# Recurrence queries, two sparse-attention projections and eight gate tiles by seven products, their weight sums on GpSimd

## The reference, cut to what matters

```python
(sq, sk, sv, dq, dk, dv, iq, ik, iw, hq, hf, hi, hg,
 g_sb, g_dsa, g_hg) = jnp.split(h @ w_in_l, _split_points(), axis=-1)
y_sb = stick_breaking_attention(heads(sq, N_SB), heads(sk, N_SB), heads(sv, N_SB)) @ w_sb_l   # 6 heads of 64
y_dsa = dsa_attention(q, k, dv, q_i, k_i, iw) @ w_dsa_l        # 64 best keys of each query, by a score of 8 index heads
o = hgrn2(heads(hq, N_HG), heads(hf, N_HG), heads(hi, N_HG), lb)   # recurrence, 4 heads; q = silu(hq), f = lb + (1 - lb) sigmoid(hf)
y_hg = (rms_norm(o, onorm) * silu(hg)) @ w_hg_l
mixed = sigmoid(g_sb) * y_sb + sigmoid(g_dsa) * y_dsa + sigmoid(g_hg) * y_hg
return mixed @ w_out_l
```

## Time and profile before

| | us |
|---|---|
| median of 3 runs | 1598.62 (1598.06 to 1599.4) |
| the profiled execution | 1599.52 |
| its span, first to last instruction | 1597.7 |
| TensorE busy | 1465.1 (92%) |
| VectorE, ScalarE, GpSimd busy | 740.9, 314.8, 22.7 |
| mixer of layer 0, from the first "hf" product | 79.8 to about 249 |
| mixer of layer 1 | about 552 to 719 |
| mean granted TensorE clock | 0.957 |

### The profile page before, as it was taken

How to read it: one execution, slowest core, us unless ns; L and a number is a source line. 1 busy time by engine, 2 the same in 40 slices (tenths; PEclk the granted TensorE clock), 3 DMA queues, 4 the chain that set the end, 5 groups by cost and what they waited for, 6 DMA issues and landing times.

```text
span 1597.7 us, 19690 instructions
## 1 busy us (share of the span) xinstructions
PE 1465.1 (92%) x8156; PEld 1006.0 (63%) x8156; DVE 740.9 (46%) x1465; ACT 314.8 (20%) x655; POOL 22.7 (1%) x41
## 2 busy tenths in 40 slices
PE   8999999999999999999999999999999576576578
PEld 5587889999544788898999445755554133133132
DVE  3646576766666646567666656544331000001001
ACT  2234431122001125430222001334410000000000
POOL 0000000000000000000000002200000000000000
PEclk9999999999999999999999999999999788788789
DMA  9547224454443633334444446755799999999997
GB/s 321 187 159 237 95 101 153 161 182 179 158 167 110 218 130 135 106 106 158 158 161 181 186 158 196 232 185 184 288 381 425 427 427 425 428 427 426 427 419 313
DMA packets 114921, 380.17 MB, mean 238 GB/s; under 512 B 10836, under 2 KB 23252, under 8 KB 104144
## 3 DMA queue, kind: packets, MB, share of 16 engines
q1 hardware_dynamic: 111952, 369.53, 60.7%
q0 software_dynamic: 2880, 9.36, 1.9%
HBM read 377.25 MB, written 5.73 MB: 240 GB/s over the span
## 4 chain that ended last, share of the span: by engine, by line
PE 32%; DMA 17%; SPq 1%; DVE 0%; ACT 0%; issue 0%; DVEq 0%
DMA ring<-in_w 17%; PE bank L1495 6%; PE bank L1541 6%; PE bank L1151 4%; PE bank L1692 4%; PE bank L1261 2%; PE bank L1590 2%; PE bank L1718 1%; SPq L928 1%; PE bank L1751 1%; PE bank L1187 1%; PE bank L1213 1%; PE bank L1200 1%; PE bank L1714 1%; PE bank L1648 0%; PE bank L1681 0%
## 5 line engine op out<-in xcount | busy, mean ns | idle before, releaser
L1144 PE MATMUL bank<-hT,ring 128*128 128x256 f32 x832 | 185.4, 381 | 0.0
L1144 PEld LDWEIGHTS bank<-hT,ring 128*128 128x128 f32 x832 | 156.0, 190 | 21.9 <-issue 1.0
L1692 PE MATMUL bank<-ring,region 128*32 128x512 f32 x208 | 115.7, 720 | 50.2 <-DMA region<-in_w 50.2
L1692 PE MATMUL bank<-region 128*32 128x512 f32 x512 | 115.8, 720 | 42.9 <-DMA ring<-in_w 42.9
L1541 PE MATMUL bank<-region 128*128 128x512 f32 x320 | 140.6, 592 | 0.0
L1541 PEld LDWEIGHTS bank<-region 128*128 128x128 f32 x320 | 60.5, 190 | 74.6 <-issue 74.6
L1495 PE MATMUL bank<-region 128*128 128x128 f32 x768 | 100.5, 275 | 0.0
L1495 PEld LDWEIGHTS bank<-region 128*128 128x128 f32 x768 | 93.0, 192 | 0.0
L1692 PEld LDWEIGHTS bank<-region 128*32 128x32 f32 x512 | 28.8, 129 | 87.4 <-issue 87.4
L1692 PEld LDWEIGHTS bank<-ring,region 128*32 128x32 f32 x208 | 25.7, 129 | 85.0 <-issue 85.0
L1751 PE MATMUL bank<-region 128*32 128x512 f32 x192 | 61.9, 748 | 15.7 <-DMA hT<-in_w 13.9
(11 more groups left out here) (486 smaller groups left out, 2413.7 us busy)
## 6 DMA issues: line engine op xcount, KB each, us to landing
region<-in_w SPq DMA_DIRECT2D x43, 2048.0 KB, 38.6
ring<-in_w SPq DMA_DIRECT2D x30, 2048.0 KB, 37.5
ring<-in_w_in SPq DMA_DIRECT2D x26, 2048.0 KB, 8.4
ring<-in_w_up SPq DMA_DIRECT2D x16, 2048.0 KB, 8.3
ring<-in_w_down SPq DMA_DIRECT2D x32, 1024.0 KB, 6.4
own_slot<-in_w SPq DMA_DIRECT2D x7, 2048.0 KB, 43.5
ring<-in_w_out SPq DMA_DIRECT2D x6, 2048.0 KB, 7.8
region<-in_w SPq DMA_DIRECT2D x22, 512.0 KB, 9.0
```

What stands on the lines that cost most here:

```text
L1144: t = mm(b[:, 0:T], w[:, k, :], act[:, k, :], start=(k == 0), stop=(k == KD - 1))
L1692: t = mm(b[32 * e:32 * e + 32, :], xg[:, k, 32 * e:32 * e + 32], four[e][c][:, 512 * (k % 2):512 * (k % 2) + 512], start=(k == 0), stop=(k ...
```

## The change

`hq` (two groups), `sk` and `sq` together (three groups, with `sk` as one half of the columns and `sq` as the other) and the gates 2 and 3 (four groups) are made by seven products. That leaves eight plain gate tiles a layer. `em` is one product of such an early group, `ec` ScalarE's copy of m1 and VectorE's four sums, `ef` what is then made of the corners. All early groups share one tile of corners in the own slot. The weight sums of all 13 groups (the late gates too) are made by GpSimd, in order, in two sets of tiles by turns, a set when the group two before is done. In the levels, 0, 2, 4 and 6 now hold a group each and level 1 one plain tile; 3 and 5 hold none. `ge` makes the tokens' sums for the gates 2 and 3 behind `ln`. `attT` is cleared behind the second `tk` and no longer in `hp`. GpSimd's sums of the first five groups stand ahead of its t5 and bias transfers, the others behind.

```diff
-LATE_GATES = 8
+PLAIN_GATES, LATE_GATES = 8, 8
+GROUPS = (("hq", 0), ("hq", 1), ("skq", 0), ("skq", 1), ("skq", 2),
+          (2, 0), (2, 1), (3, 0), (3, 1), (4, 0), (4, 1), (5, 0), (5, 1))
+EARLY, IN_HEADS = 9, 5
+POOL_SUM = {"m5": 1, "m6": 3, "m7": 3, "m3": 4}
...
+    def em(n):
+        return [("em", n, m) for m in GATE_ORDER] + [("ec", n), ("ef", n)]
...
-    s += gm("hf", 1, *GATE_ORDER) + [("gc", "hf", 1), ("gf", "hf", 1), ("hq", 0)]
-    s += [("rt", c) for c in range(9)] + [("hj",)] + [("hq", m) for m in range(1, 4)]
+    s += gm("hf", 1, *GATE_ORDER) + [("gc", "hf", 1), ("gf", "hf", 1)]
+    s += [("rt", c) for c in range(9)] + [("hj",)] + em(0) + em(1)
     s.append(("hp",))
     half = N_IDX // 2
-    s += [("ix", 0, j) for j in range(half)] + [("sk", 0)] + [("ix", 0, j) for j in range(half, N_IDX)] + [("tk", 0)]
-    s += [("sk", m) for m in (1, 2)] + [("sq", m) for m in range(3)] + [("t5",)]
+    s += [("ix", 0, j) for j in range(half)] + em(2) + [("ix", 0, j) for j in range(half, N_IDX)] + [("tk", 0)]
+    s += em(3) + em(4) + [("t5",)]
     s += [("ix", 1, j) for j in range(N_IDX)] + [("tk", 1)]
-    s += [("z", c) for c in range(3)] + g(2) + [("ln",)] + g(2)
+    s += [("z", c) for c in range(3)] + g(2) + [("ln",), ("ge",)] + g(2)
...
-        s += g(2 if j < 2 else 1)
-
-    s += [("gt",), ("gw", 4), ("ho",)]
+        s += em(5 + j // 2) if j % 2 == 0 else g() if j == 1 else []
+
+    s += [("gt",), ("ho",)]
...
+            def weight_sums(l, n):
+
+                G = nc.gpsimd
+                for c in {"hq": ("hq",), "skq": ("sk", "sq")}.get(GROUPS[n][0], (("g", GROUPS[n][0]),)):
+                    pool.wait_ge(*arrive[chunk_at[(l, c)]])
+                if n == 0:
+                    pool.wait_ge(*bk.full((l, "rsb")))
+                elif n == 1 and l == 0:
+                    pool.wait_ge(kv_stored, 16)
+                elif n >= 2:
+                    pool.wait_ge(*group_done(l, n - 2))
+                (a11, a12), (a21, a22) = group_weights(l, n)
+                s1, s2, s3, s4 = group_sums(l, n)
+                at = 4 * (len(GROUPS) * l + n)
+                G.tensor_tensor(s1, a21, a22, ALU.add).then_inc(pool_sums, 1)
+                G.tensor_tensor(s3, a11, a21, ALU.subtract).then_inc(pool_sums, 1)
+                pool.wait_ge(pool_sums, at + 1)
+                G.tensor_tensor(s2, s1, a11, ALU.subtract).then_inc(pool_sums, 1)
+                pool.wait_ge(pool_sums, at + 3)
+                G.tensor_tensor(s4, a12, s2, ALU.subtract).then_inc(pool_sums, 1)
...
+                    elif kind == "ec":
+                        A_(early_corners[:, 6, :], read((l, "ey", s[1]))[:, 0:P], ACT.Copy).then_inc(early_m1, 1)
...
+            def early_corner_sums(l, n):
+
+                if EARLY * l + n >= 1:
+                    dve.wait_ge(early_done, EARLY * l + n)
+                if 2 * l < EARLY * l + n and n in (1, 2):
+                    dve.wait_ge(hq_made, 2 * l + n)
+                x_, y_ = read((l, "ex", n)), read((l, "ey", n))
+                eight = early_corners.rearrange("p (a b) t -> p a b t", a=2)
+                pairs = early_corners.rearrange("p (a b) t -> p a b t", b=2)
+                m5, m4 = y_[:, P:2 * P], y_[:, 2 * P:3 * P]
+                dve.wait_ge(early_m1, EARLY * l + n + 1)
...
+                free(V.tensor_tensor(early_corners[:, 2, :], early_corners[:, 5, :], m4, ALU.subtract), (l, "ey", n))
...
-                        if l == 0:
-                            dve.wait_ge(kv_stored, 16)
-                        link(V.memset(attT, 0.0))
...
+                        if i == NT - 1:
+                            link(V.memset(attT, 0.0))
...
-                    elif kind == "gw":
-                        gate_weight_sums(l, s[1])
```

More of the change, by code:

```diff
@@ L186 @@
 SEVENS = ("hf", 4, 5)
+POOL_SUM = {"m5": 1, "m6": 3, "m7": 3, "m3": 4}
 GATE_STARTS, GATE_ENDS = {"m1": "gy", "m2": "gx"}, {"m3": "gx", "m4": "gy"}
 def mixer_steps():
-    gates = iter([("g", m) for m in range(24 - LATE_GATES)])
+    gates = iter([("g", m) for m in range(PLAIN_GATES)])
     def g(n=1):
         return [next(gates) for _ in range(n)]
+    def em(n):
+        return [("em", n, m) for m in GATE_ORDER] + [("ec", n), ("ef", n)]
     def gm(c, t2, *products):
@@ L1074, in _ @@
                            ).then_inc(na_stored, 16)
+            for n in range(IN_HEADS, len(GROUPS)):
+                weight_sums(0, n)
+            for n in range(len(GROUPS)):
+                weight_sums(1, n)
             pool.wait_ge(na_stored, 16)
@@ L1309, in gate_product, with early_product @@
                 b = psum[bk.bank((l, {"ux": "gx", "uy": "gy"}[name], c, t2))][:, P * place:P * place + P]
+                at = P * t2 if n < 0 else 0
                 for k in range(4):
-                    t = mm(b, left[:, k, P * t2:P * t2 + P], right[:, k, :], start=(k == 0), stop=(k == 3))
+                    t = mm(b, left[:, k, at:at + P], right[:, k, :], start=(k == 0), stop=(k == 3))
                 if m in GATE_ENDS:
                     full(t, (l, GATE_ENDS[m], c, t2))
+            def early_product(l, n, m):
+                (a11, a12), (a21, a22) = group_weights(l, n)
+                (b11, b12), (b21, b22) = h_quarters()
+                s1, s2, s3, s4 = group_sums(l, n)
+                r1, r2, r3, r4 = [gate_rows_sums[0 if n < IN_HEADS else 2][:, j] for j in range(4)]
+                left, right = {"m1": (a11, b11), "m2": (a12, b21), "m3": (s4, b22), "m4": (a22, r4),
+                               "m5": (s1, r1), "m6": (s2, r2), "m7": (s3, r3)}[m]
+                if m == "m1":
+                    for c in {"hq": ("hq",), "skq": ("sk", "sq")}.get(GROUPS[n][0], (("g", GROUPS[n][0]),)):
+                        arrived((l, c))
+                elif m == "m5" and n == IN_HEADS:
+                    pe.wait_ge(row_sums_ready, 3 * l + 2)
+                if m in POOL_SUM:
+                    pe.wait_ge(pool_sums, 4 * (len(GROUPS) * l + n) + POOL_SUM[m])
+                name, place = UP_PLACE[m]
+                key = (l, {"ux": "ex", "uy": "ey"}[name], n)
+                if m in GATE_STARTS:
+                    bank_of(key)
+                b = psum[bk.bank(key)][:, P * place:P * place + P]
+                for k in range(4):
+                    t = mm(b, left[:, k, :], right[:, k, :], start=(k == 0), stop=(k == 3))
+                if m in GATE_ENDS:
+                    full(t, key)
             pe.wait_ge(first_loaded, 16)
@@ L1342, in _ @@
                 wait_freed([(l, "rsb")])
+                rows = [slice(HD * hh, HD * hh + HD) for hh in range(2)]
                 for s in MIX:
@@ L1357, in _ @@
                         full(t, key)
-                    elif kind in FM:
-                        rows = [slice(HD * hh, HD * hh + HD) for hh in range(2)]
-                        if s[1] == 0:
-                            w = arrived((l, kind))
-                        feature_major(key, w[:, :, P * s[1]:P * s[1] + P], hT)
+                    elif kind == "em":
+                        early_product(l, s[1], s[2])
                     elif kind == "t5":
@@ L1373, in _ @@
                         c = s[1]
-                        wait_freed([(l, n, c) for n in ("sq", "sk")])
+                        pe.wait_ge(early_done, EARLY * l + c + 3)
                         b = [bank_of((l, "z", 2 * c + hh)) for hh in range(2)]
```

108 lines of the change are left out of this document (77 added, 31 removed).

## The result

The changed kernel took 1687.57 us (1686.49 to 1688.43, four runs) against 1598.34 us (1597.58 to 1599.4) for the one before on the same chip: a ratio of 1.0555, 95% interval 1.0543 to 1.0568. It is 89 us slower. The prediction had the sign right and the size wrong: +36.9 us, a range that ended at 1656, and the time lies 32 us beyond it.

The account below looks back on a forecast made before the run. TensorE was taken to bound it to about 1200 us, then expert weights' transfers. Level waits 32.7, saving -5.7, ahead of the levels +4.9, clock +5: +36.9 us on 1598.6, so 1635 us, range 1610 to 1656.

Parts of the forecast that it names:

- TensorE's waits by the order of VectorE's stream: Levels: `lm` queued behind `ec`, fillers gone, +16.3 us a layer; ahead of the levels, +4.9 in all with saving included.
- saving of the products: Nine groups by seven products in each of two layers, 0.71 us saved a group: -12.8 us in all.
- slow clock behind these waits: Levels: ten waits of 2.8 to 4 us may lower TensorE's clock; bounds 0 and 17, three taken, +5 us.
- the shared port, with the clock behind it: VectorE and GpSimd blocking each other on SBUF inputs, at `lm`; left out of the sum, by the rule some 9 us more.
- The walk of the order: VectorE's in-order stream followed step by step through both mixers, giving +32.7 us in the levels and +4.9 ahead of them.
- the chain E + 2.15: Behind each group's end E, ScalarE's copy and four VectorE sums: banks come free and VectorE goes on 2.15 us later.
- the silence behind the mixers: After the two layers' mixers nothing changes but the start; time lost there reaches the end in full.
- rival C: GpSimd's sums become the bound, from 8 us a group on; 64 us of waits, to 1690; chance 0.05.
- A: Waits in the levels are there but half of 32.7 us, no clock loss: 1613 us; chance 0.13.
- D: Faster: TensorE stays the bound without waits in the levels, only the 12.8 us saving is left: 1586; chance 0.05.
- rival B: Shared port: `lm` instructions wait for GpSimd sums, 1.5 us a place, 12 us more: 1648 to 1660; chance 0.22.

Follow-up runs that it names:

- short-sums row: Changed kernel with GpSimd's four sums of each group in layer 1 narrowed to 2 of every 128 columns, products on stale sums; 1663.51 us, ratio 1.0413.
- the sums held back: Changed kernel with GpSimd's sums of groups 7, 8 and 9 waiting for VectorE's `lm`, group 10's for the late gates' row sums; 1669.26 us, ratio 1.0442.

## Why the prediction was wrong

For one layer, the prediction's terms beside what layer 1 shows:

| term, us a layer | forecast | measured |
|---|---|---|
| TensorE's waits by the order of VectorE's stream | 16.3 + 6.0 = 22.3 | 20.3 |
| saving of the products | -6.4 | -4.4 |
| slow clock behind these waits | 2.5 | 6.1 |
| the shared port, with the clock behind it | 0 | 22.9 |
| sum | 18.4 | 44.9 |

(6.0 is the 4.9 / 2 ahead of the levels without the saving of 3.55 that it contains. The measured waits are the short-sums row less before's: 22.0 - 1.7. The saving is 164.9 - 160.5, at no clock lost in either. The clock is what is then left of busy: 166.6 - 160.5. The port is 211.5 - 188.6.)

**The walk of the order was right.** Without GpSimd's sums the level waits are 2.88, 2.51, 3.69, 2.67 and 3.01 us; forecast were 3.2, 2.8, 4.0, 3.0 and 3.5. Places, releasers, the chain E + 2.15 and the silence behind the mixers came out. The waits for a PSUM bank ahead of groups 2 and 3 were forecast at 1.5 each and are 1.47 and 1.48 with short sums. GpSimd takes 5.1 us a group, as taken, and TensorE never waits for it: rival C is out, and so are A and D.

**The step that failed is the port.** "The sum does without this; by the rule it would be some 9 us more", and rival B at +12 us with a chance of 0.22. B's mechanism is what happened, and what it would show (`lm` over 1 us) is in the rows. It was left out of the sum because no row of before showed it; but GpSimd had done nothing there but issue transfers, so no row could have. And it was priced too low in three ways. It took "one GpSimd instruction (about 1.1 us, the transfer row) at most of three" for each `lm`, 1.5 us at a place; the three instructions took turns with three sums, and each place cost 2.7 (4.1 instead of 1.36 us of `lm`). It counted only `lm`: the row sums of gates 4 and 5 (TensorE waits 2.6 to 2.9 us there, none with short sums), `hp` (2.32 us instead of 1.38) and the product behind `ef` also meet sums, for the same reason, that sums n + 2 start when group n ends. And its lower price carried no clock: idle 13.9 us and slower work 9.0 us make the 22.9. The idle part can be read wait by wait in layer 1, changed kernel against short sums: 8.2 us at the three `lm` behind groups, 2.1 ahead of group 3 (3.59 against 1.48), 2.6 at gate 4, and 1.2 in two waits ahead of the levels.

**The clock was the second.** "I take three" places of 1.7 us; the bounds were 0 to 17 for both layers. The waits of 2.5 to 3.7 us cost 6.1 a layer, inside those bounds. Those of over 5 us did more: with them the clock lost is 22.2 instead of 10.2 us a layer. The two terms aren't independent: the port made the waits longer, and longer waits slowed what comes behind. (The Trainium skill, TensorE: Matmul & The Clock Gate, in its part on the clock gate, says that the slow level is what TensorE falls to when it isn't kept busy. The rows agree: 0.50 behind 5.6 us without work, 1.00 in the same stretch with products in it.)

**The saving** came out at 4.4 of 6.4 us. Two groups in a row take 12.6 us here (97.72 to 110.32 in layer 0), so 0.66 us each and 5.9 in all is what the products give; the last 1.5 us are open.

What stays open besides: how the 9.0 us of slower work divide by place. The short sums took all of them away at once, and the sums held back (1669.26) moved the conflict on to two other levels.

Some side sums of the prediction slip, without weight for the forecast. Rival A adds 4 where the term is 4.9. Rival C's 64 us on top of 1635 would be 1699, not 1690, and its 12 us a group would be some four times VectorE's 0.69 us a sum, not five.

## What to carry to other kernels

Where work goes to an engine that was silent, the trace of before can't show its conflicts: put the price of the shared port into the sum for every VectorE instruction with its inputs in SBUF that the new instructions will run beside, and find these by asking what event releases the new work, since that is also what releases VectorE's. Price a wait of TensorE with the clock behind it: in layer 1 here 36 us of idle time made the products 15 us slower (175.6 against 160.5). And a saving on a filler has to be weighed against the cover that it gives to others: 4.4 us of products less cost over 20 us of waits.

## What the runs showed of the hardware

- Two instructions with their inputs in SBUF, one on each of VectorE and GpSimd, don't run side by side but take turns: 0.42 us became 1.03 to 1.48, 0.69 became 1.74, and in the reverse case GpSimd's pair of 128x512 went from 2.21 to 3.21 us. VectorE's TENSOR_SCALAR, with one tensor from SBUF, is held up too (128x1024 in 0.69 us, and 1.63 beside GpSimd's sums); corner sums with an input from PSUM aren't.
- GpSimd takes 1.27 us for one of these sums of 128x512, VectorE 0.69 us for an operation of that size with two inputs.
- TensorE with more work can be faster: 5.6 us more busy time in a layer's mixer, and 11 us less in its length.
